# The attention's branch product in three split passes, ordered behind the matrix memory's

## What is computed

```python
cols = jnp.einsum('btd,dc->btc', xn, P['w_in'][l])
...
merged = (gates[:, :, 0] * (h_a @ P['w_branch_a'][l])
          + gates[:, :, 1] * (h_b @ P['w_branch_b'][l])
          + gates[:, :, 2] * (h_c @ P['w_branch_c'][l]))
mix = (merged @ P['w_out'][l]).astype(x.dtype)
```

## Time and profile before

| | |
|---|---|
| runs shown | median 2446.35 us, 2445.53 to 2447.68 (3 runs) |
| the profiled execution, its own time | 2449.73 us |
| its span, first to last instruction | 2447.9 us |
| mean granted TensorE clock | 0.977 of full speed |
| TensorE busy | 2335.9 us, 95% |
| VectorE / ScalarE / POOL busy | 994.4 / 863.1 / 786.7 us |

### The profile page before, as it was taken

The page is one execution under the profiler, slowest core; times in us unless marked ns, Lnnn a source line. Parts: engine busy times, 40 slices in busy tenths (PEclk is TensorE's granted clock), DMA queues, the critical chain, the costliest instruction groups (busy, mean ns, idle before and its releaser), DMA issues.

```text
span 2447.9 us, 53310 instructions
## 1 busy us (share of the span) xinstructions
PE 2335.9 (95%) x23450; PEld 2224.4 (91%) x23450; DVE 994.4 (41%) x1559; ACT 863.1 (35%) x1442; POOL 786.7 (32%) x630
## 2 busy tenths in 40 slices
PE   7999989999999899999989999999999989999997
PEld 7998878988899899999989988888888989999997
DVE  4435654454434522220073376455443624332102
ACT  4345532213344522222244455222313544222222
POOL 3432322112235244444424332221212433444441
PEclk9999989999999999999989999999999999999998
DMA  5432211111124132233325221112113242332331
GB/s 164 128 88 74 57 40 32 28 49 32 42 69 145 58 90 87 87 91 87 83 93 136 61 74 53 32 28 49 32 28 83 68 129 61 90 92 87 88 88 52
DMA packets 334190, 180.80 MB, mean 74 GB/s; under 512 B 33528, under 2 KB 330648, under 8 KB 332936
## 3 DMA queue, kind: packets, MB, share of 16 engines
q1 hardware_dynamic: 333776, 177.34, 26.1%
q10 hardware_dynamic: 184, 0.05, 0.0%
HBM read 167.98 MB, written 9.38 MB: 72 GB/s over the span
## 4 chain that ended last, share of the span: by engine, by line
PE 82%; DVE 11%; ACT 4%; issue 2%; DMA 1%; POOL 0%; DVEq 0%; ACTq 0%; SPq 0%; POOLq 0%
PE psum_products L658 72%; PE psum_mixer L658 8%; DVE xn_low L2050 1%; DMA w_raw<-in_w_in 1%; DVE merged L2044 1%; DVE squares L1641 1%; DVE gate_product L2042 1%; DVE xn_low L1638 0%; ACT c_in_rate L1222 0%; ACT w_high L1222 0%; ACT c_kprime L1222 0%; DVE c_kappa_r L1753 0%; DVE c_in_rate L1754 0%; ACT L1222 0%; PE psum_mixer L1037 0%
## 5 line engine op out<-in xcount | busy, mean ns | idle before, releaser
L2273 POOL TENSOR_TENSOR w_low<-w_raw,w_high 128x512 fp32r<-128x512 f32 (+2 forms) x606 | 761.8, 1279 | 1557.7 <-ACT w_high L1222 1557.1
L658 PE MATMUL psum_products<-xn_high,w_high 128*128 128x272 f32 (+1 forms) x3424 | 738.6, 297 | 28.8 <-DVE xn_low L1623 12.3
L658 PE MATMUL psum_products<-xn_high,w_low 128*128 128x272 f32 (+1 forms) x3424 | 710.7, 289 | 0.0
L658 PE MATMUL psum_products<-xn_low,w_high 128*128 128x272 f32 (+1 forms) x3424 | 708.9, 289 | 0.0
L658 PEld LDWEIGHTS psum_products<-xn_high,w_high 128*128 128x128 f32 x3424 | 542.9, 189 | 50.6 <-issue 26.2
L658 PEld LDWEIGHTS psum_products<-xn_low,w_high 128*128 128x128 f32 x3424 | 543.0, 190 | 0.0
L658 PEld LDWEIGHTS psum_products<-xn_high,w_low 128*128 128x128 f32 x3424 | 539.7, 190 | 0.0
L1222 ACT ACTIVATE w_high<-w_raw 128x1024 fp32r<-128x1024 f32 (+2 forms) x303 | 303.2, 1003 | 174.6 <-PE psum_products L658 144.3
L658 PE MATMUL psum_products<-hidden_high,w_high 128*128 128x272 f32 x704 | 145.9, 288 | 0.0
L658 PE MATMUL psum_products<-hidden_high,w_low 128*128 128x272 f32 x704 | 145.7, 288 | 0.0
L658 PE MATMUL psum_products<-hidden_low,w_high 128*128 128x272 f32 x704 | 145.1, 288 | 0.0
(11 more groups left out here) (374 smaller groups left out, 3008.9 us busy)
## 6 DMA issues: line engine op xcount, KB each, us to landing
w_raw<-in_w_in SPq DMA_DIRECT2D x112, 512.0 KB, 4.0
w_raw<-in_w_ffn_in SPq DMA_DIRECT2D x88, 512.0 KB, 3.8
w_raw<-in_w_ffn_out SPq DMA_DIRECT2D x32, 512.0 KB, 3.9
w_raw<-in_w_out SPq DMA_DIRECT2D x16, 512.0 KB, 4.0
w_raw<-in_w_ffn_out SPq DMA_DIRECT2D x16, 384.0 KB, 3.4
x_kept<-x SPq DMA_DIRECT2D x2, 2176.0 KB, 7.5
x<-x_kept SPq DMA_DIRECT2D x2, 2176.0 KB, 9.7
w_raw<-in_w_in SPq DMA_DIRECT2D x16, 256.0 KB, 3.9
```

The lines of the kernel that those rows point to most:

```text
L658: return pe.matmul(out, lhsT, rhs, start=start, stop=stop, skip_group_check=True)
L2273: low_ready.inc(pool.tensor_tensor(wl[:, n % NSPLIT, ks_], wraw[:, slot, ks_], wh[:, n % NSPLIT, ks_].bitcast(F32), ALU.subtract))
```

## The change

The attention's branch units are split like all others. Its heads `bh` get a high part, which is written where the matrix memory's high part was (`a_high`), and a low part in a new buffer `b_low` that starts at the address of `b_heads` itself. So the high part can't be written until all eight branch units of the matrix memory are done: the order of the units becomes gates and branches of b = 0 for all m, then of b = 1. A new item `b_out_split` stands in the plan behind `branch(0,7)`: ScalarE waits for that product and copies four high parts, VectorE subtracts four times. `branch(1,0)` waits for the last of these. There are 32 fillers in place of 31, since the new item is one of them.

```diff
--- before.py
+++ after.py
@@ -163,7 +163,7 @@
 
 
 WEIGHT = {"c_prep": 1.0, "c_keys": 1.0, "c_scaled": 0.3, "c_scale": 1.0, "c_gram": 0.7, "c_level": 0.3, "c_chain": 0.5,
-          "c_state_out": 0.0, "a_chunk": 0.6, "a_chunk_out": 0.5, "a_out_split": 0.0, "a_state_out": 0.0, "a_state_put": 0.0, "b_put": 0.0, "c_shift_put": 0.0, "c_state_put": 0.0, "a_scale": 0.3, "a_out": 0.2, "b_values": 0.5,
+          "c_state_out": 0.0, "a_chunk": 0.6, "a_chunk_out": 0.5, "a_out_split": 0.0, "b_out_split": 0.0, "a_state_out": 0.0, "a_state_put": 0.0, "b_put": 0.0, "c_shift_put": 0.0, "c_state_put": 0.0, "a_scale": 0.3, "a_out": 0.2, "b_values": 0.5,
           "b_scores": 0.6, "b_out": 0.6}
 
 
@@ -182,7 +182,7 @@
 
 def gate_order():
 
-    return [(b, m) for m in range(KD) for b in range(2)] + [(2, m) for m in range(KD)]
+    return [(b, m) for b in range(3) for m in range(KD)]
 
 
 GATES = gate_order()
@@ -230,6 +230,7 @@
         products = []
         for b, m in GATES[:2 * KD]:
             products += [("gate", l, b, m), ("branch", l, b, m)]
+            products += [("b_out_split", l)] if (b, m) == (0, KD - 1) else []
         products = products[1:]
         plan += weave(c, products)
         finish = [("c_gate_in", l)] + [("c_variance", l, f) for f in range(4)]
@@ -253,7 +254,7 @@
 
 
 def unsplit(s):
-    return s[0] == "branch" and s[2] == 1
+    return False
 
 
 EARLY = (0, 1, 2, 16, 3, 4)
@@ -394,6 +395,8 @@
     bh_at = (max(w.end(), a_rb_at + 4 * KD * T) + 63) // 64 * 64
     w = worker(bh_at)
     bh = w("b_heads", [P, 4, T])
+
+    b_low = place("b_out_low", [P, 4, T], bh_at, F32R)
 
     rest = (w.end() + 63) // 64 * 64
     w = worker(rest)
@@ -719,7 +722,7 @@
                     if b == 0:
                         gemm(s, rh=a_high, rl=a_low, nk=4, steps=steps)
                     elif b == 1:
-                        gemm(s, rhs=[bh[:, k, :] for k in range(4)], nk=4, steps=steps)
+                        gemm(s, rh=a_high, rl=b_low, nk=4, steps=steps)
                     else:
                         gemm(s, rh=c_high, rl=c_low, nk=4, steps=steps)
                 else:
@@ -1171,14 +1174,14 @@
                     norm_pre(*s[1:])
                 elif kind == "norm_post":
                     norm_post(*s[1:])
-                elif kind in ("norm_late", "a_out_split", "bias_put", "bias_get", "a_log", "a_state_put", "b_put", "c_shift_put", "c_state_put"):
+                elif kind in ("norm_late", "a_out_split", "b_out_split", "bias_put", "bias_get", "a_log", "a_state_put", "b_put", "c_shift_put", "c_state_put"):
                     pass
                 elif kind in ("cols_c", "cols_a", "cols_b", "gate", "ffn_gate", "ffn_up", "branch"):
                     if kind == "branch" and s[3] == 0:
                         if s[2] == 0:
                             flow("a_h").wait_next(pe, "pe")
                         elif s[2] == 1:
-                            bank[2].wait_emptied(pe, ("b_out", s[1], 8))
+                            flow("b_h").wait_next(pe, "pe")
                         else:
                             flow("c_h").wait_next(pe, "pe")
                     product(s)
@@ -1388,6 +1391,11 @@
             def c_finish(l, f):
                 flow("c_out").wait_next(act, "act")
                 step(fn(c_high[:, f, 0:T], cc[:, f, 0:T], ACT.Copy), flow("c_out_high"))
+
+            def b_out_high(l):
+                act.wait_ge(products.sem, unit_no[("branch", l, 0, KD - 1)] + 1)
+                for h in range(4):
+                    step(fn(a_high[:, h], bh[:, h, :], ACT.Copy), flow("b_out_high"))
 
             def a_out_high(l):
                 flow("a_out").wait_next(act, "act")
@@ -1578,7 +1586,7 @@
                      "c_keys": c_keys, "c_scaled": c_scaled, "a_norm": a_norm,
                      "c_state_out": c_state_out, "c_gate_in": c_gate_in, "c_variance": c_variance, "c_rsqrt": c_rsqrt, "c_finish": c_finish,
                      "a_chunk_out": a_chunk_out, "c_chain": c_chain,
-                     "a_rows": a_rows, "a_chunk": a_chunk, "a_tokens": a_tokens, "a_out_split": a_out_high, "a_log": a_log, "a_state_out": a_state_out,
+                     "a_rows": a_rows, "a_chunk": a_chunk, "a_tokens": a_tokens, "a_out_split": a_out_high, "b_out_split": b_out_high, "a_log": a_log, "a_state_out": a_state_out,
                      "b_values": b_values, "b_out": b_out,
                      "merge_split": merge_split}[kind](*s[1:])
                 for n in ahead.get(s, ()) if kind != "norm_post" else ():
@@ -1975,6 +1983,11 @@
                      bank[3].empty["dve"])
                 if g == GROUPS - 1:
                     step(dve.tensor_copy(stats[0:1, 61:62], stats[0:1, 61:62]), flow("a_out"))
+
+            def b_out_low(l):
+                for h in range(4):
+                    flow("b_out_high").wait_next(dve, "dve")
+                    step(tt(b_low[:, h, :], bh[:, h, :], a_high[:, h].bitcast(F32), SUB), flow("b_h") if h == 3 else None)
 
             def a_out_low(l):
                 for h in range(4):
@@ -2110,7 +2123,7 @@
                      "c_scale": c_scale, "c_keys": c_keys, "c_scaled": c_scaled, "a_norm": a_norm,
                      "c_gate_in": c_gate_in, "c_variance": c_variance,
                      "a_chunk_out": a_chunk_out, "a_out": a_out, "a_scale": a_scale,
-                     "a_rows": a_rows, "a_chunk": a_chunk, "a_tokens": a_tokens, "a_out_split": a_out_low, "a_log": a_log, "b_values": b_values, "b_scores": b_scores,
+                     "a_rows": a_rows, "a_chunk": a_chunk, "a_tokens": a_tokens, "a_out_split": a_out_low, "b_out_split": b_out_low, "a_log": a_log, "b_values": b_values, "b_scores": b_scores,
                      "b_out": b_out}[kind](*s[1:])
 
 
```

## The result

The changed kernel takes 2464.97 us (median of 4 runs, 2464.08 to 2465.90), the kernel before in the same job 2447.01 us. The ratio is 1.0066, with a 95% interval from 1.0053 to 1.0079: slower by 0.66%. The forecast was 2451.4, its range ended at 2461.

The account below looks back on a forecast made before the run. TensorE's queue, busy for 95% of the span, was taken as the bound. Product -13.0, idle +14.2 and clock +3.2 sum to +4.4 us: 2450.8 from the 2446.35 median, put at 2451.4; range 2440 to 2461.

Parts of the forecast that it names:

- The product: Attention's 16 units in three passes, each giving back 0.87 us of TensorE work: 13.0 us saved in both layers.
- 15 fragments: Attention steps run in pieces between mixer matmuls, about 15 a layer, each giving back some 0.1 us less.
- The idle: TensorE waits in the mixer's five groups grow from 22.1 to 29.2 us a layer: +14.2 in both layers.
- the wait behind the gram: Group 2, TensorE without filler waits for a longer VectorE queue at the gram: 1.9 us, between 0.9 and 3.4.
- those of the levels: Group 2, three levels without filler, where TensorE waits for VectorE's masks: 3.1 us together.
- Elsewhere: Extra splits on ScalarE and POOL, merges moved to the second half: no cost, 2 us either way in the range.
- the clock: One added fall to half clock in each layer, ahead of `c_kprime` in group 2: +3.2 us, ends -3 and 9.
- The faster rival: Evenly made splits end POOL's bursts, shortening VectorE's queue ahead of `c_kprime` in groups 0 to 3: 2441 us; chance 0.16.
- Half clock through the bare stretch: Rival: 1.2 GHz through group 2's gram and three levels without filler, 10.4 us more a layer: 2472 us; chance 0.08.
- Late weights: Rival: split attention units wait for `w_low`, so the 13 us are gone: 2464 us; chance 0.03.
- The signs for being right: Three passes at 0.75 us a step; some 11 us idle in layer 0's group 2; about 1 us a level.
- the tie: Rival: group 2's stretch without filler costs 4.0 us, group 1 hides its 0.7, no clock falls more: 2444.2; chance 0.28.

Follow-up runs that it names:

- POOL is held: POOL starts no low parts between its `c_rk` product and VectorE's last operation ahead of `c_kprime`: changed kernel 2442.54 us, kernel before 2443.86, the product alone 2432.89.
- The order alone: Changed kernel with its new order of units, but the attention's units unsplit as before and no split of its heads: 2464.99 us, ratio 1.0066.
- the product alone: Kernel before, old order, with the attention's units in three split passes on the matrix memory's heads (result not the program's): 2457.32 us, ratio 1.0035.

## Why the prediction was wrong

**The product** (-13.0) was right or a little high: -11.8 alone in the work column, some -10 with the estimate below the budget, and -11.0 us of time once POOL is held. Its own terms come to less than 13.0: 15 fragments in each of two layers at 0.1 us are 3.0, and 13.9 - 3.0 + 0.7 is 11.6. The order alone reads 3.2 us less work (623.1 to 619.9) where fewer fragments were to bring 0.7; with a column that differs by 4.4 among equal products, that isn't shown to be the fragments.

**The idle** (+14.2) came out at +17.7, and the sum looks better than its parts, since errors cancel. Group 2 has 8.96 us in layer 0 and 9.97 in layer 1 for 11.1: the wait behind the gram is 1.10 for 1.9, those of the levels 1.03, 0.87 and 0.86, together 2.8 for 3.1. Groups 1 and 3 fit in number, but there waits for `c_kprime` of 3.28 and 3.29 us stand where before part was waiting for `w_low`. Group 0 kept 1.83 of its wait for `c_kprime` in place of 1.0. Group 4 has the wait that I didn't see: 2.71 us, from POOL's burst on VectorE, 6.86 us of idle for 5.0. With POOL held in both kernels, the change's idle is +8.2 (33.9 to 42.1): the +14.2, worked out almost without POOL, came near +17.7 in part by luck.

**The step that failed first** is "Elsewhere": "POOL has the room", "Nothing for these". Busy share was the wrong question. POOL's subtractions cost by when they run: beside VectorE's last four operations ahead of `c_kprime` they make these up to 4.4 times as long. I had the row for it (1.64 for 0.69 us), charged 0.7 in group 1, took 0.9 off in group 2 and left the rest. In group 4, where nothing was charged for it, the four operations went from 1.16 to 3.89 us. Holding POOL takes 16.3 us of idle and 12.4 of the clock's loss from the kernel after; from the kernel before it takes 6.7 of idle and none of the clock's loss. The term that stood at nothing is the difference.

**The step that was mis-sized** is the clock, +3.2 with ends -3 and 9: +11.4. One fall more in each layer was counted, in group 2; 1.6 us each by the earlier trace rows. By the same budget, over both layers and a fifth too high like its sum, about 7.5 us came in group 2, 6.1 in group 4 and 1.2 in group 1, and group 0 lost 3.2 less, the low end that the prediction gave. Group 4 lost nothing before; its loss stands beside the new wait of 2.71 us. The length of a wait alone doesn't say where it falls: group 3's wait for `c_kprime` grew from 2.40 to 3.29 us and its loss stayed as it was.

**The rivals and signs.** The faster rival turned on the same mechanism and was argued against correctly, since the operations of L1753 to L1756 stayed at 1.1 us and more in the full groups, but for the last one in group 2 (0.69); I didn't give it the other sign. Half clock through the bare stretch held in part: 1.2 GHz at 514.77, full clock again at 520.09, with 5.2 and 4.0 us lost in group 2 where the rival had 12 in each layer. Late weights did not come: `w_low` fell from 15.0 to 6.0 us. What none of them said is that the product's gain might itself turn into waits, as the product alone showed at 2457.32 us. The signs for being right came nearly all (three passes, 9 to 10 us of idle in group 2 under the names given, waits of about 1 us a level): they looked at the order's cost, and the miss lay elsewhere. The three chances of within, slower and faster (0.39, 0.43, 0.18) don't follow from the five given: half of 0.45 with the tie's 0.28 is some 0.5 within, and the rest leaves 0.34 slower and 0.16 faster.

## What to carry to other kernels

Before a cheaper product is credited, ask what will be late when it ends sooner: 11.8 us of work was saved here and the kernel got slower until the helper engine was told to stay away from the critical chain. Try such a cure on the kernel before as well: here it brought a quarter as much there, and showed that the change itself was worth nothing in time. An engine at 33% can still set the time, through operations of another engine that run beside it; look at the durations of the same operation with and without company, and try a wait on the helper before moving any work. And price a new wait with the clock that may fall behind it.

## What the runs showed of the hardware

- A VectorE product with both inputs in SBUF, 128x128, took 0.29 us alone and up to 1.27 beside POOL's subtractions; 128x512 took 0.69 and up to 1.67. With POOL held, three of the four operations came to 0.69 in every full group; the first stayed at up to 1.67, beside POOL's own product for `c_rk`.
- Twelve matmuls that nobody reads, in each of ten waits, made one kernel 12.7 us faster and another not at all. Stretches at 1.2 GHz stood beside many of the longer waits, but not all of them and not only these.
